# Modulation products of a two-block model move from the expert layer to two feed-forward layers

## Chip, cores and metric

The kernel runs on one core of a Trainium2 chip. The time is device microseconds of one execution, from its first to its last instruction with what lies around it; several executions are run and their median is given. Lower is better.

## What is computed

The reference runs two blocks over 256 tokens of 1024 features. The first block has two layers (attention, convolution, then a dense feed-forward in layer 0 and 8 routed experts in layer 1). The second block has two layers, and each of its steps is modulated by vectors that are made from two conditions, `c` for the tokens and `c_ctx` for a context of 256 tokens:

```python
silu_c = jax.nn.silu(c)
silu_cc = jax.nn.silu(c_ctx)
for i in range(DEPTH):
    m_lat = jnp.split((silu_c @ w_mod[i] + b_mod[i])[:, None, :], N_MOD, axis=-1)
    m_ctx = jnp.split((silu_cc @ w_mod[i] + b_mod[i])[None, None, :], N_MOD, axis=-1)
    h_lat = ffn_sublayer(h_lat, m_lat[0], m_lat[1], m_lat[2], ...)
    ...
```

`w_mod[i]` is 1024 x 9216 fp32 for each of the two layers, 75 MB together. It depends on nothing that the first block computes, so its products can stand anywhere before their first reader.

## The kernel before

Features lie on partitions, tokens on the free axis. The order of work is written out by hand, engine by engine, as a row of phases: `win0`, `proj0`, `wout0`, `ffn`, `win1`, `proj1`, `wout1`, `moe` (first block), then `fa0`, `naqkv`, `wo0`, `fb0`, `fa1`, `waqkv`, `wo1`, `fb1` (second block). Engines meet by semaphores only.

A phase is a row of steps. A step loads one weight tile of 128 x 2048 (an up step, gate and up of 128 hidden features, or any plain projection) or 128 x 1408 (a down step) by SyncE (SP) into one of four RAW slots. Each tile is cut in two pieces. ScalarE rounds a piece to fp32r (`high`, L1333, into WH), VectorE makes the rest (`low`, L1724, into WL), both two steps ahead of TensorE. TensorE multiplies three times for each block of 128 x 128 weights: high by high, low input by high weight, high input by low weight (`piece_product`, L936). An up step has 48 such products and a down step 33, of 256 columns (272 in `ffn`); steps of `fa0`, `fb0` and `fa1` that serve both streams have twice as many. `ffn` has 38 steps: two experts' worth of 11 up and 8 down steps. `moe` has 8 x 19 = 152. `fa0` and `fb0` have 65: 16 up steps of one stream, 3 up steps of both, 8 down steps of both (19 to 26), then 11 up and 8 down steps of each stream alone (27 to 45, 46 to 64).

`load` (L694) waits until VectorE has made the low part of the step four earlier, and SP issues its DMAs strictly in order. Results go to PSUM: `bank` gives a step one of four pairs of banks in turn, and `begin` makes TensorE wait until the former user of the pair is evacuated.

**The modulation.** `w_mod` is 72 tiles of 128 x 2048, 36 of each layer. `mod_product` (L977) multiplies a tile by the 2-column conditions SCF: 8 fp32 matmuls (16 records in the profile), at four column positions of the array in turn. The tiles stand beside experts 0 to 5 of `moe`, 12 beside each, in pairs behind the steps 1, 4, 7, 10, 13 and 16 of an expert (`mod_tiles`, `beside_moe`). One buffer is MRAW, the other TMP, and GpSimd loads them in a loop over the experts (L817), each when the product two tiles earlier is done (`s_mpc`). ScalarE copies the 2 x 4 result rows of a tile from PSUM to MROW (`mod_out`, L1395) and writes them to DRAM by four DMAs of 2 KB (L1398). In expert 6 ScalarE reads all 72 rows back (L1411), TensorE turns them by 16 transposes (`mod_turn`, L988), VectorE sums the four partial rows and the bias in four rounds (`mod_round`, L1785) and finishes them (`mod_finish`), and GpSimd makes the tables AB and GA of all five norms of the second block (`tables`).

Two more places matter. Between phases stands a layer norm: `norm` on TensorE sums over features by products with ONES (L1092, L1098). And norms of the second block are "hosted" by phases (`half_norm`, `half_sum`): beside steps 0 to 7 of `fa0`, 46 to 53 of `fa0` and so on, TensorE makes one product L1029 at the first of these steps and one L1032 at the third, which waits for GpSimd's sum of squares (L867). The routing of `moe` has 16 products of 8 columns at step 1 (L1008, 32 records) and 16 of 128 columns at each of the steps 5 and 7 (L1017).

Of the kernel before, what the change touches and what calls it, by code (L numbers as in the profile page):

```python
# [28 lines left out]
P = 128  # L29
# [39 lines left out]
MOD_EXPERTS = 6  # L69
MOD_PER_EXPERT = MOD_STEPS // MOD_EXPERTS  # L70
# [60 lines left out]
class Phase:  # L131
# [187 lines left out]
def build(nc, ins, out):  # L319
# [11 lines left out]
    with ctx:  # L331
# [16 lines left out]
        MLD = TMP[0:MOD_STEPS, :, :].rearrange("p a (b n) -> p (a b) n", b=2)  # L348
# [38 lines left out]
        MTILE = [MRAW[:, :], TMP[:, :, :].rearrange("p a b -> p (a b)")]  # L387
# [267 lines left out]
        def mod_rows_of(g, st, j):  # L655


            return PS[1 + 4 * (g // 2) + 2 * j][:, (2 * (g % 2) + st) * MOD_STEPS:(2 * (g % 2) + st + 1) * MOD_STEPS]
# [30 lines left out]
        def _(sp):  # L689
# [10 lines left out]

            def in_steps(name, e0):
                p = ph[name]
                for s, (t, e, k, _) in enumerate(p.steps):
                    load(p, s, ins["w_gu" if t == "u" else "w_dn"][e0 + e, k])

            def bias_tiles(layer):


                if layer == 0:
                    sp.wait_ge(s_browd, 32)  # L710
                sp.wait_ge(s_pc, ph[f"win{layer}"].p0)
# [55 lines left out]
        def _(pool):  # L767
# [44 lines left out]
            pool.wait_ge(s_pc, ph["moe"].p0)  # L812
            pool.wait_ge(s_ul, KC * (U_IDX["moe"] + 1))
# [17 lines left out]
            def tables():  # L831

                named = [hn for hn in halves if hn.half == 0]

                for hn in named:
                    t = (hn.layer * 72 + hn.idx * KC) // 2
                    for st in range(2):
                        sh = MOD[:, st, t:t + KC // 2, :].rearrange("p a b -> p (a b)")
# [4 lines left out]
                pool.wait_ge(s_tab, 10)  # L843
# [46 lines left out]
            pool.wait_ge(s_mod, 10)  # L890
            tables()
# [17 lines left out]
            for name in ("2n0", "2b0", "2a1"):  # L909
                two_halves(name)  # L910
# [4 lines left out]
        def _(pe):  # L915
# [54 lines left out]
            def mod_product(i, k):  # L970


                pe.wait_ge(s_mev, i * MOD_PER_EXPERT + k + 1)
                pe.wait_ge(s_mw[k % 2], (i * (MOD_PER_EXPERT // 2) + k // 2 + 1) * 16)
                for b in range(2):
                    for g in range(4):
                        last = pe.matmul(PS[1 + 2 * (k % 2)][32 * g:32 * g + 2, 0:256], SCF[:, 4 * b + g, :],  # L977
# [3 lines left out]
            def mod_turn():  # L981

                pe.wait_ge(s_mrl, 16)
                pe.wait_ge(s_mev, MOD_STEPS + 2)
# [7 lines left out]
            def beside_moe(i, s):  # L992


                if i < MOD_EXPERTS:
                    for k in mod_tiles(s):
                        mod_product(i, k)
                elif i == MOD_EXPERTS and s == 3:
                    mod_turn()
# [44 lines left out]
            def in_steps(name):  # L1044
# [4 lines left out]
                for s, (t, e, k, (c0, n)) in enumerate(p.steps):  # L1049
# [16 lines left out]
                    if name == "moe":  # L1066
# [1219 lines left out]
```

## Time and profile before

| | |
|---|---|
| median of 3 timed runs | 3238.85 us |
| lowest and highest of them | 3236.56, 3258.69 us |
| profiled execution, its own time | 3272.8 us |
| its span, first to last instruction | 3271.1 us |
| TensorE busy | 3160.7 us, 97% |
| VectorE, ScalarE, GpSimd busy | 1945.0, 1578.4, 392.3 us |
| mean granted TensorE clock | 0.987 |

The durations below are from the one profiled execution. Lines are those of the kernel before. PE is TensorE, PEld its weight loads, DVE VectorE, ACT ScalarE, POOL GpSimd, SP SyncE. A `q` behind an engine's name marks what its sequencer issues, such as a DMA. Products are pipelined: each record is about 0.28 us long, and one starts about every 0.12 us, so the distance from start to start is what a product costs.

### The profile page before, as it was taken

What the parts mean: (1) busy time and instruction counts of PE and PEld (TensorE: products, weight loads), DVE (VectorE), ACT (ScalarE), POOL (GpSimd) and SP (SyncE); (2) the same over time, 40 slices, a digit from 0 to 9 for tenths busy, and PEclk for the clock granted to TensorE, in tenths of its full rate; (3) what the DMA queues carried; (4) which work ended last, traced back from release to release, by engine and by line L of the source; (5) the groups of instructions that cost most, each with busy time, mean ns of one, the idle gap of its engine ahead of it and who ended that gap; (6) DMA issues with size and microseconds to landing.
All of it is one profiled execution on the core that took longest, in us unless ns stands there. A gap on an engine that the chain in (4) does not pass through costs nothing.

```text
span 3271.1 us, 63095 instructions
## 1 busy us (share of the span) xinstructions
PE 3160.7 (97%) x26594; PEld 3031.7 (93%) x26594; DVE 1945.0 (59%) x3076; ACT 1578.4 (48%) x2707; POOL 392.3 (12%) x482
## 2 busy tenths in 40 slices
PE   8999999999999999999999999999999999998998
PEld 7789998898889989999999997889999999996998
DVE  5965569645545555667357645584467635776554
ACT  4654455544444444455245546553355524556544
POOL 0000040000000000122001412150011400130000
PEclk9999999999999999999999999999999999999999
DMA  6335482367777787555245541243455424550352
GB/s 245 116 116 174 165 260 104 120 253 285 293 284 273 289 305 260 196 190 183 95 155 192 195 173 41 102 163 110 151 181 198 169 97 160 186 185 26 125 191 97
DMA packets 102866, 580.81 MB, mean 178 GB/s; under 512 B 16977, under 2 KB 25297, under 8 KB 49658
## 3 DMA queue, kind: packets, MB, share of 16 engines
q1 hardware_dynamic: 86176, 489.54, 42.2%
q0 software_dynamic: 13568, 84.91, 7.0%
q8 instruction: 211, 3.46, 0.4%
q10 hardware_dynamic: 2842, 2.34, 0.2%
q14 instruction: 69, 0.57, 0.0%
HBM read 575.08 MB, written 11.04 MB: 179 GB/s over the span
## 4 chain that ended last, share of the span: by engine, by line
PE 82%; DVE 9%; ACT 3%; DMA 2%; POOL 2%; issue 1%; ACTq 0%; POOLq 0%; SPq 0%; DVEq 0%
PE PS L936 73%; DVE CONV L2054 3%; DVE WL L1724 2%; PE PS L1218 2%; DMA TMP<-in_w_mod 2%; PE PS L977 2%; POOL TMP L867 1%; PE PS L1191 1%; PE PS L1205 1%; ACT WH L1333 1%; PE PS L1098 1%; PE PS L1092 1%; DVE NMX L1953 0%; DVE RSTD L1743 0%; DMA RAW<-in_w_in 0%
## 5 line engine op out<-in xcount | busy, mean ns | idle before, releaser
L1724 DVE TENSOR_TENSOR WL<-RAW,WH 128x1024 fp32r<-128x1024 f32 (+1 forms) x1018 | 1157.6, 1140 | 909.2 <-ACT WH L1333 902.3
L936 PE MATMUL PS<-UH,WH 128*128 128x256 f32 (+1 forms) x5536 | 1536.0, 284 | 24.8 <-DVE TMP L2114 7.8
L936 PE MATMUL PS<-UL,WH 128*128 128x256 f32 (+1 forms) x5536 | 1521.8, 281 | 0.0
L936 PE MATMUL PS<-UH,WL 128*128 128x256 f32 (+1 forms) x5536 | 1521.4, 281 | 0.0
L1333 ACT ACTIVATE WH<-RAW 128x1024 fp32r<-128x1024 f32 (+1 forms) x1018 | 982.5, 968 | 886.2 <-PE PS L936 865.3
L936 PEld LDWEIGHTS PS<-UH,WH 128*128 128x128 f32 x5536 | 1038.6, 190 | 41.9 <-issue 18.1
L936 PEld LDWEIGHTS PS<-UH,WL 128*128 128x128 f32 x5536 | 1034.6, 190 | 0.0
L936 PEld LDWEIGHTS PS<-UL,WH 128*128 128x128 f32 x5536 | 1033.6, 189 | 0.6
L936 PE MATMUL PS<-HIDH,WH 128*128 128x256 f32 (+1 forms) x2112 | 550.8, 281 | 0.0
L936 PE MATMUL PS<-HIDL,WH 128*128 128x256 f32 (+1 forms) x2112 | 548.4, 280 | 0.0
L936 PE MATMUL PS<-HIDH,WL 128*128 128x256 f32 (+1 forms) x2112 | 548.4, 280 | 0.0
L936 PEld LDWEIGHTS PS<-HIDH,WH 128*128 128x128 f32 x2112 | 381.4, 190 | 8.7 <-issue 6.5
L936 PEld LDWEIGHTS PS<-HIDL,WH 128*128 128x128 f32 x2112 | 380.4, 189 | 0.0
L936 PEld LDWEIGHTS PS<-HIDH,WL 128*128 128x128 f32 x2112 | 380.2, 189 | 0.0
L1468 ACT ACTIVATE SILHT<-PS 128x256 f32<-128x256 f32 (+2 forms) x255 | 99.3, 389 | 358.6 <-PE PS L936 358.5
L1890 DVE TENSOR_TENSOR SILHT<-SILHT,PS 128x256 f32<-128x256 f32 (+2 forms) x255 | 109.8, 431 | 217.8 <-ACT SILHT L1468 217.8
L1471 ACT ACTIVATE HIDH<-SILHT 128x256 fp32r<-128x256 f32 (+2 forms) x255 | 107.1, 420 | 19.4 <-DVE SILHT L1890 18.9
L1896 DVE TENSOR_TENSOR HIDL<-SILHT,HIDH 128x256 fp32r<-128x256 f32 (+2 forms) x255 | 116.2, 456 | 0.0
L856 POOL TENSOR_TENSOR TMP<-H 128x256 f32<-128x256 f32 x9 | 7.1, 790 | 846.4 <-DVE H L1837 823.4
L817 POOL DMA_DIRECT2D MRAW<-in_w_mod x36 | 19.1, 530 | 714.1 <-PE PS L977 551.7
L2054 DVE SCALAR_TENSOR_TENSOR CONV<-HPAD,VEC,CONV 128x272 f32<-128x272 f32 (+1 forms) x232 | 96.5, 486 | 0.0
L1837 DVE SCALAR_TENSOR_TENSOR H<-PS,MOD,H 128x256 f32<-128x256 f32 x128 | 58.6, 479 | 44.3 <-PE PS L936 44.3
(207 smaller groups left out, 2280.6 us busy)
## 6 DMA issues: line engine op xcount, KB each, us to landing
RAW<-in_w_gu SPq DMA_DIRECT2D x255, 1024.0 KB, 4.8
RAW<-in_w_dn SPq DMA_DIRECT2D x168, 704.0 KB, 4.1
MRAW<-in_w_mod POOLq DMA_DIRECT2D x36, 1024.0 KB, 7.0
TMP<-in_w_mod POOLq DMA_DIRECT2D x36, 1024.0 KB, 9.6
RAW<-in_w_in SPq DMA_DIRECT2D x30, 1024.0 KB, 8.0
RAW<-in_w_na SPq DMA_DIRECT2D x20, 1024.0 KB, 4.9
RAW<-in_w_o SPq DMA_DIRECT2D x12, 1024.0 KB, 4.8
RAW<-in_w_proj SPq DMA_DIRECT2D x8, 1024.0 KB, 4.9
```

What stands on the lines that cost most here:

```text
L867: pool.tensor_tensor(s2, s2, TMP[:, slot, at], ALU.add).then_inc(s_s2p, 1)
L936: last = pe.matmul(ps[:, a:b], w, m[:, a:b], start=first and a == 0, stop=final and b == n)
L977: last = pe.matmul(PS[1 + 2 * (k % 2)][32 * g:32 * g + 2, 0:256], SCF[:, 4 * b + g, :], MTILE[k % 2][:, (4 * b + g) * 256:(4 * b + g + 1) ...
L1218: last = pe.matmul(out, PT2[:, 2 * (g % 2) + half, x * P:(x + 1) * P], QKV[:, a.value0 + a.chunk(it), j * P + HD * half:j * P + HD * half ...
L1333: act.activation(WH[slot][:, 0:hi - lo], RAW[:, p.raw(s), lo:hi], ACT.Copy).then_inc(s_hi, 1)
L1468: act.activation(SIL[:, k % 2, 0:n], pair_banks(p, s)[0], ACT.Silu).then_inc(s_sil, 1)
L1471: act.activation(HIDH[:, k, hid_cols((c0, n))], HT[:, k % 2, 0:n], ACT.Copy).then_inc(s_hid, 1)
L1724: dve.tensor_tensor(WL[slot][:, 0:hi - lo], RAW[:, p.raw(s), lo:hi], WH[slot][:, 0:hi - lo].bitcast(F32), ALU.subtract).then_inc(s_lo, 1)
L1837: last = dve.scalar_tensor_tensor(x, ps[:, t0 - r[0]:t0 - r[0] + nt], mod(*gate, m, st), x, ALU.mult, ALU.add)
L1890: dve.tensor_tensor(HT[:, k % 2, 0:n], SIL[:, k % 2, 0:n], pair_banks(p, s)[1], ALU.mult).then_inc(s_evd, 1)
L1896: dve.tensor_tensor(HIDL[:, k, cols], HT[:, k % 2, 0:n], HIDH[:, k, cols].bitcast(F32), ALU.subtract).then_inc(s_hidl, 1)
L2054: own.inc(dve.scalar_tensor_tensor(y, x, tap, y, ALU.mult, ALU.add))
```

## The change

The 36 tiles of layer 0 now stand beside `ffn`, one behind each of its steps 1 to 36. The 36 tiles of layer 1 stand beside `fa0`, one behind a step, from step 22 on; where a down step serves one stream, the steps 1, 3 and 5 of the eight have none (and none is left for the last, 7, of the second stream). SP loads them, each behind the weight load of four steps later (`mod_load`). Their buffers are MRAW and CB (the router's weights, not in use in those phases); TMP is no longer one. In `ffn` the results go to banks 6 and 7, so the steps of `ffn` share three pairs of banks instead of four; in `fa0` they go to banks 1 and 3. TensorE waits for the last copy of layer 0 before the norm `b0`, which follows `ffn`.

The rows are turned per layer: ScalarE reads 36 of them back at step 19 of `moe` (expert 1) and at step 19 of `fb0`; TensorE turns them at step 22 by 16 products with the identity, which now add up the four partial rows in PSUM; VectorE adds the bias in two instructions and finishes five of the groups (`mod_sum`). GpSimd makes the tables of layer 0's three norms behind the first turn, and those of layer 1's two norms between the norms `2n0` and `2b0`. Waits are moved to match. The load loop on GpSimd is gone.

```diff
+MOD_LAYER = MOD_STEPS // 2
+MOD_FROM = {"ffn": 1, "fa0": 22}
+MOD_LOAD_LAG = 4
+MLD_STEP, TURN_STEP = {"moe": 19, "fb0": 19}, {"moe": 22, "fb0": 22}
...
+        if self.name == "ffn":
+            return 2 * (s % (BANK_SETS - 1))
...
-        MTILE = [MRAW[:, :], TMP[:, :, :].rearrange("p a b -> p (a b)")]
+        MTILE = [MRAW[:, :], CB[:, :, :].rearrange("p a b -> p (a b)")]
+        MLD = MRAW[0:MOD_LAYER, :].rearrange("p (b n) -> p b n", b=8)
...
-        def mod_tiles(s):
-            return (2 * (s // 3), 2 * (s // 3) + 1) if s % 3 == 1 and s < 18 else ()
+        def mod_steps(name):
+            steps = [(s, t, k, r) for s, (t, _, k, r) in enumerate(ph[name].steps) if s >= MOD_FROM[name]]
+            if name == "fa0":
+                steps = [x for x in steps if x[1] == "u" or x[3] == BOTH or x[2] not in (1, 3, 5)]
+            return [x[0] for x in steps[:MOD_LAYER]]
...
+        def mod_bank(k):
+            return PS[6 + k % 2] if k < MOD_LAYER else PS[1 + 2 * (k % 2)]
...
+            def mod_load(k):
+                if k == 0:
+                    sp.wait_ge(s_pc, ph["ffn"].p0)
+                if k == MOD_LAYER:
+                    sp.wait_ge(s_mrt, 1)
+                    sp.wait_ge(s_evd, ph["moe"].evacs("d", ph["moe"].n))
+                sp.wait_ge(s_mpc, k + 1)
+                sp.dma_start(MTILE[k % 2], ins["w_mod"][k]).then_inc(s_mw[k % 2], 16)
...
                 for s, (t, e, k, _) in enumerate(p.steps):
                     load(p, s, ins["w_gu" if t == "u" else "w_dn"][e0 + e, k])
+                    tile = mod_tile(name, s - MOD_LOAD_LAG)
+                    if tile is not None:
+                        mod_load(tile)
+                for s in range(p.n - MOD_LOAD_LAG, p.n):
+                    if mod_tile(name, s) is not None:
+                        mod_load(mod_tile(name, s))
...
-            with pool.Fori(0, MOD_EXPERTS) as i:
-                for k in range(MOD_PER_EXPERT):
-                    pool.wait_ge(s_mpc, i * MOD_PER_EXPERT + k + 1)
-                    pool.dma_start(MTILE[k % 2], ins["w_mod"][i * MOD_PER_EXPERT + k]).then_inc(s_mw[k % 2], 16)
...
-                for j in range(2):
-                    for g in range(4):
-                        for st in range(2):
-                            last = pe.transpose(mod_rows_of(g, st, j), MLD[:, 2 * g + st, j * P:(j + 1) * P],
-                                                IDENT[0:MOD_STEPS, 0:MOD_STEPS])
+                for g in range(4):
+                    for st in range(2):
+                        for j in range(2):
+                            last = pe.matmul(mod_rows_of(st, j), MLD[:, 2 * g + st, j * P:(j + 1) * P],
+                                             IDENT[0:MOD_LAYER, 0:MOD_LAYER], start=g == st == j == 0,
+                                             stop=g == 3 and st == j == 1)
...
+            def mods(name, s):
+                if mod_tile(name, s) is not None:
+                    mod_product(mod_tile(name, s))
+                if TURN_STEP.get(name) == s:
+                    mod_turn(int(name == "fb0"))
...
                 in_steps(nm)
                 if i == 0:
+                    pe.wait_ge(s_mev, MOD_LAYER + 2)
                     norm("b0", H, ONES, c0, n, s_evd, lambda c: ph[nm].evacs("d") - KC + c + 1)
```

How the order changes, at three places. First TensorE in the experts before: behind step 1 stand the router's products (L1008) and the first pair of tiles (L977, one from MRAW, one from TMP); the next pair stands three steps later.

```order
L936 MATMUL PS<-UL,WH 128x256
L936 MATMUL PS<-UH,WL 128x256
L1008 MATMUL PS<-RT,H 128x8 x16
L977 MATMUL PS<-MRAW,SCF 2x256 x8
L977 MATMUL PS<-TMP,SCF 2x256 x8
L936 MATMUL PS<-UH,WH 128x256
...
L936 MATMUL PS<-UH,WL 128x256
L977 MATMUL PS<-MRAW,SCF 2x256 x8
L977 MATMUL PS<-TMP,SCF 2x256 x8
L936 MATMUL PS<-UH,WH 128x256
```

In the changed kernel (where L936 is L971, L977 is L1012, L1008 is L1042, L1017 is L1051 and the turn is L1022) the tiles stand in `ffn`, one behind a step. The first two are these, from MRAW and from CB:

```order
L971 MATMUL PS<-UH,WL 128x272
L1012 MATMUL PS<-MRAW,SCF 2x256 x8
L971 MATMUL PS<-UH,WH 128x272
...
L971 MATMUL PS<-UH,WL 128x272
L1012 MATMUL PS<-CB,SCF 2x256 x8
L971 MATMUL PS<-UH,WH 128x272
```

In the experts the router's products are left with L971 on both sides; further on stand the routing's products at step 5 and the turn of layer 0.

```order
L971 MATMUL PS<-UH,WL 128x256
L1042 MATMUL PS<-RT,H 128x8 x16
L971 MATMUL PS<-UH,WH 128x256
...
L971 MATMUL PS<-UH,WL 128x256
L1051 MATMUL PS<-CST,STD 128x128 x4
L1051 MATMUL PS<-CST,RSTD 128x128 x4
L971 MATMUL PS<-UH,WH 128x256
...
L971 MATMUL PS<-UH,WL 128x256
L1022 MATMUL PS<-CST,MRAW 128x36 x16
L971 MATMUL PS<-UH,WH 128x256
```

So no tile is left in the experts, and each tile now has 33 to 96 products of L971 on either side instead of another tile on one.

The third place is SP's queue at `ffn`. Before, its loads of gate and up weights (`in_w_gu`), down weights (`in_w_dn`) and then those of `win1` (`in_w_in`) stand alone:

```order
L694 DMA RAW<-in_w_out 128x2048 x4
L694 DMA RAW<-in_w_gu 128x2048 x11
L694 DMA RAW<-in_w_dn 128x1408 x8
L694 DMA RAW<-in_w_gu 128x2048 x11
L694 DMA RAW<-in_w_dn 128x1408 x8
L694 DMA RAW<-in_w_in 128x2048 x9
```

Now (L714 is `load`, L730 `mod_load`) a tile stands behind each weight load from the sixth on, and four behind the last:

```order
L714 DMA RAW<-in_w_out 128x2048 x4
L714 DMA RAW<-in_w_gu 128x2048 x6
L730 DMA MRAW<-in_w_mod 128x2048
L714 DMA RAW<-in_w_gu 128x2048
L730 DMA CB<-in_w_mod 128x2048
...
L714 DMA RAW<-in_w_dn 128x1408
L730 DMA MRAW<-in_w_mod 128x2048
L730 DMA CB<-in_w_mod 128x2048
L730 DMA MRAW<-in_w_mod 128x2048
L730 DMA CB<-in_w_mod 128x2048
L714 DMA RAW<-in_w_in 128x2048 x9
```

The loads of `fa0` read alike from its step 26 on. SP takes them in this order only, so a weight load now also stands behind what the tile ahead of it waits for.

## Rows read from the trace of the kernel before

**Rows 1.** The page, engines and the chain by line.

```profile
PE 3160.7 (97%) x26594; PEld 3031.7 (93%) x26594; DVE 1945.0 (59%) x3076; ACT 1578.4 (48%) x2707; POOL 392.3 (12%) x482
...
PE PS L936 73%; DVE CONV L2054 3%; DVE WL L1724 2%; PE PS L1218 2%; DMA TMP<-in_w_mod 2%; PE PS L977 2%; POOL TMP L867 1%; PE PS L1191 1%; PE PS L1205 1%; ACT WH L1333 1%; PE PS L1098 1%; PE PS L1092 1%; DVE NMX L1953 0%; DVE RSTD L1743 0%; DMA RAW<-in_w_in 0%
```

**Rows 2.** Waits of the whole span (us in total, times, longest).

```profile
PE PS L977 <- DMA TMP<-in_w_mod: 11.3, 5, 2.7
...
PE PS L1032 <- POOL TMP L867: 12.5, 9, 1.5
```

**Rows 3.** Timeline, TensorE around one pair of modulation tiles (start us, us, engine line).

```profile
1023.30 1.04 PE L977 MATMUL PS<-MRAW,SCF 128*2 128x256 f32 x16
...
1024.16 1.05 PE L977 MATMUL PS<-TMP,SCF 128*2 128x256 f32 x16
...
1025.13 0.19 PEld L936 LDWEIGHTS PS<-UH,WH 128*128 128x128 f32 x1 [0.44 <-issue]
1025.14 0.38 PE L936 MATMUL PS<-UH,WH 128*128 128x256 f32 x1
```

**Rows 4.** The chain in order of time (start us, us, what).

```profile
238.22 192.90 PE PS L936 x1560
...
1004.99 1.84 PE PS L977 x32
...
1023.37 1.84 PE PS L977 x32
...
1310.44 163.29 PE PS L936 x1440
1487.12 268.55 PE PS L936 x2280
```

**Rows 5.** Windows with a low clock: stretch, busy us (instructions) by engine, PEclk, DMA share, GB/s.

```profile
660.80:664.20 3.40, 3.40 (x33) 1.08 (x32) 0.00 (x0) 0.00 (x0) 0.53 (x1) 0.50 0.88 316
753.00:756.40 3.40, 3.40 (x23) 2.01 (x23) 0.00 (x0) 0.00 (x0) 0.53 (x1) 0.50 1.00 342
964.60:968.00 3.40, 3.15 (x22) 1.77 (x23) 0.00 (x0) 0.00 (x0) 0.53 (x1) 0.50 0.94 301
1176.20:1179.60 3.40, 3.40 (x19) 3.36 (x16) 0.00 (x0) 0.00 (x0) 0.53 (x1) 0.50 0.96 366
```

**Rows 6.** Windows with the products of L936 alone.

```profile
757.00:774.50 17.50, 17.50 (x151) 1.00 0.74 271
777.00:792.50 15.50, 15.50 (x139) 1.00 0.77 280
969.00:986.00 17.00, 17.00 (x147) 1.00 0.74 274
989.00:1004.50 15.50, 15.50 (x140) 1.00 0.75 277
```

**Rows 7.** Timeline: the turn of before and the router's products.

```profile
657.19 3.63 PE L1008 MATMUL PS<-RT,H 128*128 128x8 f32 x32
...
1309.26 1.18 PE L988 MATMUL PS<-CST,TMP 72*128 72x72 f32 x16
```

**Rows 8.** Windows: the kernel's first loads.

```profile
4.00:14.00 10.00, 5.36 (x16) 4.20 (x16) 1.33 (x2) 3.29 (x3) 0.00 (x0) 1.00 1.06 408
```

**Rows 9.** DMA issues (KB each, median us to landing).

```profile
RAW<-in_w_gu SPq DMA_DIRECT2D x255, 1024.0 KB, 4.8
RAW<-in_w_dn SPq DMA_DIRECT2D x168, 704.0 KB, 4.1
...
TMP<-in_w_mod POOLq DMA_DIRECT2D x36, 1024.0 KB, 9.6
```

**Rows 10.** Timeline: the end of ffn.

```profile
430.96 1.31 PE L1092 MATMUL PS<-H,ONES 128*128 128x272 f32 x5
431.16 1.06 ACT L1333 ACTIVATE WH<-RAW 128x1024 fp32r<-128x1024 f32 x1 [0.73 <-PE PS L936]
```

**Rows 11.** Instructions of line L1395 (duration ns min/median/max).

```profile
L1395 ACT ACTIVATE MROW<-PS x72: 360/383/396, 673.6 to 1286.6; 128x256 f32<-128x256 f32 x72
```

More of the change, by code:

```diff
@@ L710, in bias_tiles @@
                     sp.wait_ge(s_browd, 32)
+                else:
+                    for b in range(2):
+                        sp.wait_ge(s_mr[b], MOD_LAYER // 2 * 64 + 16)
                 sp.wait_ge(s_pc, ph[f"win{layer}"].p0)
@@ L829, in modulate, with tables @@
                     last.then_inc(s_um, 1)
-            def tables():
-                named = [hn for hn in halves if hn.half == 0]
+            def tables(layer):
+                named = [hn for hn in halves if hn.half == 0 and hn.layer == layer]
                 for hn in named:
@@ L888, in two_halves @@
                         half_residual(hn)
-            pool.wait_ge(s_mod, 10)
-            tables()
+            pool.wait_ge(s_mod, 5)
+            tables(0)
             for c in range(KC):
@@ L908, in _ @@
                 pool.tensor_tensor(nbv, nbv, mask, ALU.add).then_inc(s_nb, 1)
-            for name in ("2n0", "2b0", "2a1"):
-                two_halves(name)
+            two_halves("2n0")
+            pool.wait_ge(s_mod, 10)
+            tables(1)
+            two_halves("2b0")
+            two_halves("2a1")
             modulate("fb1", "2n1", 1, 6, SEQ)
@@ L1065, in in_steps @@
                             piece_product(p, s, h, [(PS[p.bank(s)][:, 0:n], terms, h == 0, h == 1)], part)
-                    if name == "moe":
-                        if s < KH:
-                            routing(s)
-                        beside_moe(*expert_step(s))
+                    if name == "moe" and s < KH:
+                        routing(s)
+                    mods(name, s)
                     hn, j = hosted(p, s)
@@ L1473, in in_steps @@
                         ahead(p, s)
-                    if name == "moe":
-                        if s < KH:
-                            routing(s)
-                        beside_moe(*expert_step(s))
+                    if name == "moe" and s < KH:
+                        routing(s)
+                    mods(name, s)
+                    if name == "moe" and expert_step(s)[0] == N_EXP - 1:
+                        context_input(expert_step(s)[1])
                     hn, j = hosted(p, s)
@@ L1764, in low_u @@
                 return (3 if modulated else 2), make
-            def mod_round(g):
-                if g == 0:
-                    dve.wait_ge(s_mrt, 1)
-                else:
-                    dve.wait_ge(s_dve, mod_rounds[-1])
-                for st in range(2):
-                    for j in range(2):
-                        base = MOD[:, st, :, j] if g else VEC[:, V_BM + j:V_BM + 2 * MOD_STEPS:2]
-                        own.inc(dve.tensor_tensor(MOD[:, st, :, j], mod_rows_of(g, st, j), base, ALU.add))
-                mod_rounds.append(own.value)
@@ L1779, in mod_finish, with mod_sum @@
[L1779 to L1800 removed]
+            def mod_sum(layer):
+                dve.wait_ge(s_mrt, layer + 1)
+                tiles = slice(layer * MOD_LAYER, (layer + 1) * MOD_LAYER)
+                bias = VEC[:, V_BM + layer * 2 * MOD_LAYER:V_BM + (layer + 1) * 2 * MOD_LAYER].rearrange("p (t j) -> p t j", j=2)
+                for st in range(2):
+                    rows = PS[1][:, 2 * st * MOD_LAYER:2 * (st + 1) * MOD_LAYER].rearrange("p (j t) -> p t j", j=2)
+                    last = dve.tensor_tensor(MOD[:, st, tiles, :], rows, bias, ALU.add)
+                link(last)
+                for idx in (1, 4, 7, 2, 8):
+                    m = MOD[:, :, layer * 36 + idx * 4:layer * 36 + idx * 4 + 4, :]
+                    dve.tensor_scalar(m, m, *((1.0, None, ALU.add) if idx in (1, 4, 7) else (0.5, None, ALU.mult)))\
+                        .then_inc(s_mod, 1)
@@ L1801, in beside_moe, with mods, context_input @@
+            def mods(name, s):
+                if TURN_STEP.get(name) == s - 1:
+                    mod_sum(int(name == "fb0"))
+            def context_input(s):
+                if 2 <= s <= KC + 1:
                     c = s - 2
@@ L1918, in in_steps @@
                             ahead(p, s, (1,))
-                    if name == "moe":
-                        if s < KH:
-                            routing(s)
-                        beside_moe(e, s % (KH + KC))
+                    if name == "moe" and s < KH:
+                        routing(s)
+                    mods(name, s)
+                    if name == "moe" and e == N_EXP - 1:
+                        context_input(s % (KH + KC))
                     if hn:
@@ L2153, in _ @@
             in_steps("fb0", (0, 8), 6)
+            dve.wait_ge(s_mod, 10)
             in_steps("fa1", (1, 2), 8)
```

101 lines of the change are left out of this document (41 added, 60 removed).

## The prediction

> **What bounds the kernel now.** I read the page first. TensorE is busy 97% of the span, and in the chain that ended last the products of the three-term weight scheme (PE L936) alone hold 73%. Beside them the same row has two entries of the modulation: 2% in which the chain runs through "DMA TMP<-in_w_mod", 2% for the products L977 [rows 1]. So the question is what the modulation costs TensorE where it stands now and where it will stand. The waits say that TensorE really stood still for a modulation tile only 5 times, 11.3 us in all [rows 2]. The chain in order of time gives the rest. A pair of tiles recurs every three steps: one begins at 1004.99, the next at 1023.37, 18.38 us for 144 products of L936 and the pair [rows 4]. Where no modulation stands between, 1440 products take 163.29 us, 113.4 ns each [rows 4], so 144 are 16.33 us and a pair costs 2.05 us.
>
> The timeline shows what these 2.05 us are made of [rows 3]: 0.86 us from the first tile's start (1023.30) to the second's, 0.98 us from the second's start until L936 goes on at 1025.14, and the other 0.21 us ahead of the first. The weight loads stood idle for 0.44 us before L936's first one. The 0.21 and what is over 0.86 in the 0.98 belong to the change of kind, not to the tile. A pair pays it once.
>
> By the Trainium skill (TensorE: Matmul & The Clock Gate, Part 3: Packing small matmuls) a weight load runs beside products in flight only where it uses other rows of the array; these tiles use all 128, so a group has to drain. This trace agrees, with its 0.44 us. The rule speaks against splitting pairs.
>
> Two more things are read from the windows. The granted clock was 0.50 for 3.4 us at 753.0, 964.6 and 1176.2, each time at a late tile, and at 660.8, right after the 32 short products of the router, L1008 [rows 5, 7]. The other two of the five late tiles were not followed by a low clock. And L936 has two spacings at full clock: 151 in 17.5 us (116 ns) from 757.0, then 139 in 15.5 us (111.5 ns as counted) after the next pair; 147 in 17.0 from 969.0, then 140 in 15.5 [rows 6]. On long stretches these are 113.4 ns [rows 4] and 268.55/2280 = 117.8 ns, in fa0 [rows 4]. Both times the wide spacing ended at a modulation group; nothing else stood there.
>
> **The change, part by part.** All 72 tiles remain, with the same 16 recorded products each, but every one stands alone: 36 behind steps 1 to 36 of ffn, 36 behind steps of fa0. A tile alone costs 0.21 + 0.98 = 1.19 us. The bounds are half a pair, 1.03 us, and a whole pair, 2.05 us; I take 1.19, since both its parts are measured.
>
> 1. Experts (moe). 36 pairs leave: 36 x 2.05 = 73.8 us. The waits go, 11.3 us [rows 2], with three stretches of 3.4 us at half clock, 1.7 us each, 5.1 us [rows 5], and the wide spacing after two of them, some 155 products x 4.4 ns each, 1.4 us. Together -91.6 us. The half clock at 660.8 follows L1008, which stays: it will now lie on L936 at about the same price, 0. What can be late next in the experts is nothing that the trace shows: weights land in 4.8 and 4.1 us [rows 9] and have some three steps.
>
> 2. The turn. 16 transposes with one record each took 1.2 us [rows 7]. Now 16 true fp32 products stand in each of two turns. The nearest row is L1008, 16 such products with 128 weight columns, 32 records, 3.6 us [rows 7]; the bound below is the transposes' 1.2 us. I take 3.6 us each: in moe -1.2 + 3.6 = +2.4, in fb0 +3.6. L1008 was followed by a half clock; for one of the two turns I count 1.7 us (bounds 0 and 3.4).
>
> 3. ffn. 36 x 1.19 = +42.8 us. No product of L936 waits there now (192.90 us for 1560, 123.7 ns [rows 4]), so nothing of it lies under a wait. If a group ends the wide spacing here too, 1536 products go from 123.7 to 113.4 + 16/2.4 = 120.1 ns (16 columns more at 2.4 GHz): -5.5 us; bounds -5.5 and 0. I take -5.5, since two of two did so. The three bank pairs instead of four cost nothing: VectorE empties a bank during the next step, two before it is needed.
>
> 4. The end of ffn. TensorE must now see the last tile's copy before the norm b0. ScalarE makes that copy behind its last weight part, which starts at 431.16 and takes 1.06 us [rows 10]; the copy takes 0.38 us [rows 11]. With the two hand-overs between the engines the sums for the norm begin at about 432.8 instead of 430.96 [rows 10]: +1.8 us, all on the path.
>
> 5. fa0. 36 x 1.19 = +42.8 us. One wait of about 1.4 us for GpSimd's sums (12.5 us in 9, [rows 2]), behind step 48, is covered by the three groups before it: -1.4. From step 22 to the wait at step 48 the spacing is wide in the row of 2280; 1248 products x 4.4 ns = -5.5 us if a group ends it. In fb0 the turn might do the same, another -5.5 us; a turn isn't a modulation group, and I count nothing.
>
> 6. The loads. They leave GpSimd's queue for SP's, each behind the weight load of four steps later. SP reaches it about 2 us into the interval after step x-2, since that weight load waits for VectorE's part of step x. What is then queued: a tile behind a weight load. Alone they land in 4.8 us (1024 KB) and 4.1 us (704 KB) [rows 9], and the stream moved 408 GB/s while the first loads of the kernel were queued [rows 8], so 1.05 MB more take 2.6 us: 7.4 us behind an up load, 6.7 behind a down load. The time there is until the product: two steps and two groups less 2 us. In up steps of ffn (48 x 123.7 = 5.9 us) 12.2 us, in down steps (33, 4.1 us) 8.5 us. In the down steps of fa0, 3.74 us at 113.4 ns, with one group between, 6.7 us: three tiles behind up loads are late by 0.7 us. I take +1 us (0 to 3). ffn asks 1.77 MB in 5.27 us in its down steps, 336 GB/s, below the 408. SP's wait for the product before the last one holds up weights only at the end, where win1's first has a norm's time.
>
> The Trainium skill (DMA: Bandwidth & Descriptors, Specifications) gives about 358 GB/s as one core's share of HBM; the trace had 408, so the measurement decides. With 358 a tile would land 0.4 us later, which makes eight tiles in fa0's down steps late by 0.4 us more, some 3 us by an estimate from that page.
>
> GpSimd's loop goes at no gain, as it is waited for only through its loads. The table work splits in two, each several steps ahead of its reader. VectorE's sums shrink from 16 to 4 and lie beside TensorE. ScalarE copies the same 72 rows; one per step is less at a time.
>
> Sum: moe -91.6 + 2.4 = -89.2; ffn +42.8 - 5.5 + 1.8 = +39.1; fa0 +42.8 - 1.4 - 5.5 = +35.9; fb0 +3.6; turn's clock +1.7; late tiles +1.0. That is -7.9 us. The profiled execution took 3272.8 us, so 3265; it was 1.0% above the median of the timed runs, 3238.85, where the same difference gives 3231. A measurement of this kernel can tell about 1% (32 us) from no change, so I call it the same.
>
> **The rivals.**
> A. A lone group drains no worse than its half of a pair, and the turns keep the clock and close up fb0: 72 x 0.16 = 11.5, 1.7 and 5.5 us less, -26 us, 3212. For it: the mean over all the pairs. Against it: the 0.44 us idle before every return to L936.
> B, the slower side. The modulation groups are what puts the expert stream into its narrow spacing, and without them it stays wide from the half clock at 660.8 on: 6240 products x 4.4 ns = +27 us, and if groups don't close up ffn and fa0 either, +11 us. Together +31 us, 3270. It decides at the first product behind L1008's half clock. For it: both changes from wide to narrow came at such groups. Against it: the routing's products (L1017) and the turn also break the stream, within 25 us, and the spacing stayed narrow for 163 us with no group in it.
> C. Tiles come late in the queue they now share with the weights: if the second load lands in 9.6 us, as TMP's tiles did from GpSimd's queue [rows 9], 16 down steps of ffn and 9 of fa0 wait 1.1 to 2.9 us each, and a late tile can cost 1.7 us in clock. 25 x 2.5 = +62 us, 3293. Against it: 9.6 us was the second of two tiles beside weights, under an issuing loop.
> D. The change doesn't do what it says: waits remain in moe for another reason. Then -7.9 + 17.8 = +10 us, 3249.
>
> **How the numbers follow.** My forecast 0.53, A 0.15, B 0.17, C 0.10, D 0.05. Below 3206 lies only the tail of A with more gain than I can name, 0.07. Above 3271 lie C and half of B's spread with the timing's own (the three runs went to 3258.69): 0.15. The rest, 0.78, is within 1%. The range 3206 to 3272 holds A, B and D. The likeliest case's own is 3222 to 3243.
>
> **What would show it.** In the changed profile: no wait of the tile products in moe; moe shorter by 89 us; lone groups every 7.1 us in ffn, 1.19 us each in the chain; L936 near 120 ns in ffn and 113.4 in fa0 behind step 22; a norm b0 that starts 1.8 us after the last product; turns of 3.6 us. Wrong would be: tile products waiting for DMA in down steps (C), 117.8 ns through the experts (B), lone groups at 1.03 us (A), or a half clock that recurs in ffn.

## The result and the profile after

| | before | after |
|---|---|---|
| median, us | 3260.58 (16 runs, 3236.56 to 3285.67) | 3274.92 (16 runs, 3257.86 to 3298.77) |
| profiled execution, us | 3272.8 | 3264.8 |
| its span, us | 3271.1 | 3262.9 |

The ratio is 1.0053, with a 95% interval of 1.0028 to 1.0079; it is worked out without one run of before, 3285.67 us, which counts as slow, and the medians of the table alone differ by 14 us. The change costs 0.5%, about 17 us (9 to 26), where the forecast had a gain of 7.9. It lies within 1%, as the likeliest class said, but on the other side of 1, and 3275 lies above the range. Of the 44 us between 3231 and 3275 half is not the change: the kernel before, run 16 times beside the changed one, has a median 22 us above that of the three runs which the forecast started from.

The two profiled executions alone would say the opposite, since the one after is 8.2 us shorter. So the first thing to read is the page, and then the stretches that the change touches.

The page after: engines, the chain by line, DMA issues.

```profile
PE 3158.6 (97%) x26642; PEld 3018.8 (93%) x26642; DVE 1945.3 (60%) x3064; ACT 1577.8 (48%) x2707; POOL 360.8 (11%) x410
...
PE PS L971 74%; DVE CONV L2090 3%; DVE WL L1769 2%; PE PS L1251 2%; PE PS L1012 2%; PE PS L1224 1%; POOL TMP L899 1%; PE PS L1238 1%; DMA MRAW<-in_w_mod 1%; ACT WH L1367 1%; PE PS L1131 1%; PE PS L1125 1%; DVE NMX L1989 0%; DVE RSTD L1788 0%; DMA RAW<-in_w_in 0%
...
RAW<-in_w_gu SPq DMA_DIRECT2D x255, 1024.0 KB, 4.8
RAW<-in_w_dn SPq DMA_DIRECT2D x168, 704.0 KB, 4.1
MRAW<-in_w_mod SPq DMA_DIRECT2D x36, 1024.0 KB, 7.5
CB<-in_w_mod SPq DMA_DIRECT2D x36, 1024.0 KB, 7.0
```

L936 is now L971, and L977 is L1012. Against [rows 1], the modulation's transfer has gone from 2% of the chain to 1%, the products' share has stayed at 2%. TensorE is as busy as before.

The waits after:

```profile
PE PS L1066 <- POOL TMP L899: 11.5, 9, 1.5
...
PE PS L1012 <- DMA MRAW<-in_w_mod: 5.2, 4, 2.1
...
PE PS L1125 <- ACT MROW L1429: 1.4, 1, 1.4
```

Against [rows 2], 11.3 us of waiting for tiles in the experts are gone, and 5.2 us of a new kind are there, in ffn and fa0. The wait at the norm b0 is the third line.

Windows from the first product of ffn, moe, fa0 and fb0 to the first of the phase behind it (columns as in [rows 5]), before and then after:

```profile
234.63:444.77 210.14, 207.63 (x1649) 205.29 (x1649) 116.83 (x162) 100.78 (x150) 3.72 (x9) 1.00 0.51 175
645.14:1468.10 822.96, 810.74 (x7568) 761.79 (x7569) 446.56 (x676) 373.80 (x580) 69.97 (x129) 0.99 0.70 260
1468.10:1842.36 374.26, 371.51 (x3178) 370.91 (x3177) 218.46 (x296) 168.53 (x250) 42.59 (x44) 1.00 0.47 163
2133.96:2516.47 382.51, 374.82 (x3179) 373.85 (x3177) 227.72 (x309) 173.35 (x258) 61.87 (x61) 0.99 0.45 156
```

```profile
235.60:491.83 256.23, 250.44 (x2224) 218.82 (x2225) 116.69 (x162) 110.52 (x186) 3.56 (x9) 1.00 0.77 288
691.92:1430.46 738.54, 737.97 (x6432) 737.05 (x6433) 449.50 (x657) 353.62 (x508) 29.29 (x43) 0.99 0.53 186
1430.46:1841.70 411.24, 406.13 (x3754) 377.27 (x3753) 215.54 (x296) 178.01 (x285) 46.27 (x44) 1.00 0.65 241
2133.20:2517.74 384.54, 376.82 (x3211) 375.64 (x3210) 228.28 (x316) 173.29 (x258) 65.33 (x75) 0.98 0.45 156
```

The first number behind each window is its length. In this pair the four stretches grow by 0.7 us in all, while the span shrinks by 8.2: stretches that the change does not touch differ by some 9 us. That happens between executions of one kernel too: the second block's fa1 lasted from 368.8 to 377.6 us over four executions of the kernel before. A single pair of profiles can't judge a change of this size by its span; the touched stretches over several can. Each kernel was profiled four times (this run and three more each). Mean length, us:

| stretch | before (lowest to highest) | after | difference | forecast |
|---|---|---|---|---|
| ffn | 210.1 (all) | 256.3 (255.1 to 257.1) | +46.2 | +39.1 |
| moe | 820.7 (818.2 to 823.0) | 738.6 (all) | -82.2 | -89.2 |
| fa0 | 369.9 (364.1 to 374.3) | 413.2 (411.2 to 415.1) | +43.3 | +35.9 |
| fb0 | 382.0 (381.7 to 382.5) | 385.1 (382.0 to 389.6) | +3.0 | +3.6 |
| turn's clock, late tiles | | | in the rows above | +2.7 |
| sum | | | +10.3 | -7.9 |

+10.3 lies inside the timing's 9 to 26. The whole spans of the same eight profiles don't: their means are 3263.5 before and 3265.7 after, only 2.2 us apart, above all since fa1 took 365.8 to 366.1 us in all four profiles after, 8.0 less on the mean. The products of fa1 are the same in both kernels, and in lag3 and expert_groups, whose fa1 is that of the changed kernel, it took 374.7 and 374.9; whether the change has a part in it is not shown. So the account that follows is one of the touched stretches, +10.3 against -7.9, 18 us of error, and not of the whole time.

### The profile page after: what moved, and what is told of

It is laid out like the page before. It is cut to its first block, busy times and chain, and to the rows that moved or that the text cites. A ratio compares the mean times of both kernels' runs of the same rounds, so it can differ in the third digit from the quotient of the medians.

```text
span 3262.9 us, 62962 instructions
## 1 busy us (share of the span) xinstructions
PE 3158.6 (97%) x26642; PEld 3018.8 (93%) x26642; DVE 1945.3 (60%) x3064; ACT 1577.8 (48%) x2707; POOL 360.8 (11%) x410
## 4 chain that ended last, share of the span: by engine, by line
PE 83%; DVE 9%; ACT 3%; POOL 1%; DMA 1%; issue 1%; ACTq 0%; SPq 0%; POOLq 0%; DVEq 0%
PE PS L971 74%; DVE CONV L2090 3%; DVE WL L1769 2%; PE PS L1251 2%; PE PS L1012 2%; PE PS L1224 1%; POOL TMP L899 1%; PE PS L1238 1%; DMA MRAW<-in_w_mod 1%; ACT WH L1367 1%; PE PS L1131 1%; PE PS L1125 1%; DVE NMX L1989 0%; DVE RSTD L1788 0%; DMA RAW<-in_w_in 0%
## 5 line engine op out<-in xcount | busy, mean ns | idle before, releaser
L971 PE MATMUL PS<-UH,WH 128*128 128x256 f32 (+1 forms) x5536 | 1534.5, 283 | 24.3 <-DVE TMP L2150 7.8
L971 PE MATMUL PS<-UL,WH 128*128 128x256 f32 (+1 forms) x5536 | 1518.0, 280 | 0.0
L971 PE MATMUL PS<-UH,WL 128*128 128x256 f32 (+1 forms) x5536 | 1517.5, 280 | 0.0
L971 PEld LDWEIGHTS PS<-UH,WH 128*128 128x128 f32 x5536 | 1036.5, 190 | 50.3 <-issue 26.6
L971 PEld LDWEIGHTS PS<-UL,WH 128*128 128x128 f32 x5536 | 1038.2, 190 | 0.6
L971 PEld LDWEIGHTS PS<-UH,WL 128*128 128x128 f32 x5536 | 1036.4, 190 | 0.0
L971 PE MATMUL PS<-HIDH,WH 128*128 128x256 f32 (+1 forms) x2112 | 547.2, 280 | 0.0
L971 PE MATMUL PS<-HIDL,WH 128*128 128x256 f32 (+1 forms) x2112 | 543.8, 278 | 0.0
L971 PE MATMUL PS<-HIDH,WL 128*128 128x256 f32 (+1 forms) x2112 | 543.6, 278 | 0.0
L971 PEld LDWEIGHTS PS<-HIDH,WH 128*128 128x128 f32 x2112 | 378.1, 188 | 13.2 <-issue 6.6
L971 PEld LDWEIGHTS PS<-HIDL,WH 128*128 128x128 f32 x2112 | 378.5, 188 | 0.0
L971 PEld LDWEIGHTS PS<-HIDH,WL 128*128 128x128 f32 x2112 | 378.1, 188 | 0.0
L1514 ACT ACTIVATE HIDH<-SILHT 128x256 fp32r<-128x256 f32 (+2 forms) x255 | 106.9, 419 | 10.7 <-DVE SILHT L1925 10.3
L1251 PE MATMUL PS<-QKV,PT 128*128 128x64 f32 x640 | 79.4, 277 | 1.0 <-DVE OS L2054 0.9
```

What stands on the lines that cost most here:

```text
L971: last = pe.matmul(ps[:, a:b], w, m[:, a:b], start=first and a == 0, stop=final and b == n)
L1251: last = pe.matmul(out, PT2[:, 2 * (g % 2) + half, x * P:(x + 1) * P], QKV[:, a.value0 + a.chunk(it), j * P + HD * half:j * P + HD * half ...
L1514: act.activation(HIDH[:, k, hid_cols((c0, n))], HT[:, k % 2, 0:n], ACT.Copy).then_inc(s_hid, 1)
```

## The experiments

The theory at this point: lone groups cost what was forecast, but the spacing of L971 doesn't narrow at them, and tiles come late more often. The rivals: B (the experts stay wide), C (late tiles decide), and that the turns cost the rest.

**Both kernels once more.** No edit.

> The changed kernel once more, for a second profile. Spacing theory (the change's own costs come to about nothing, and the median is 17 us worse because the expert stream, without its pairs of tiles, now often stays in the wide spacing of 117.8 ns instead of 113.3): moe differs from the first profile's 738.5 us by up to 27 us, the time stays 10 to 25 us above before. Cost theory (late tiles and half clocks cost more in most executions than in the first profile): moe again 735 to 742 us, but more than 5 us of waits of tile products, or more half clocks, in ffn and fa0.

> The kernel before once more, for a second profile and as a measure of the noise. Ratio 1.000 within 0.004. Spacing theory: moe again within 5 us of 823, since a pair of tiles every three steps brings L936 back to 113.3 ns; the phases without pairs (ffn, fa0, fb0, fa1, fb1) differ from the first profile by 5 to 15 us each, one way or the other. Cost theory: those phases agree within 2 us.

After: 3271.41 us, ratio 1.0060 (1.0031 to 1.0088). Before: 3262.52 us, 1.0024 (0.9995 to 1.0054) against itself, in the same session. So 0.3% is what this measurement can give for no change. The cost of the change shows twice, but against the second build of before, measured beside it, it is 0.3% (9 us) and no more. Two further profiled executions of each filled the table above.

> The changed kernel a third time, for its profile. Spacing theory: moe between 738 and 766 us, in steps that stand with the spacing of L971 (wide 117.8, narrow 113.3 ns). Cost theory: 738 us again.

> The kernel before a third time, for its profile. If the 12 us of the median that the profiles do not show lie in the spacing of phases which the change touches, some profile of before has ffn below 207 us or fa0 below 368 us (narrow). If not, ffn 210, moe 822, fa0 374 and fb0 382 come again within 1 us each.

> The changed kernel a fourth time, for its profile. If its experts are wide in some executions, moe is above 745 us in one profile of four; if not, 738.5 us again, and the four phases of the change (ffn, moe, fa0, fb0) sum to 1790 to 1797 us again.

> The kernel before a fourth time, for its profile; expected as for the third.

They took 3263.91 and 3266.67 us after, 3266.77 and 3251.95 before. moe was 738.5 to 738.6 us in all four profiles of after, so wide experts don't explain them.

**No tiles at all** (no_tiles). The 72 loads, products and copies are left out; the turned rows come from weights, so the modulation isn't computed.

```diff
-                    tile = mod_tile(name, s - MOD_LOAD_LAG)
-                    if tile is not None:
-                        mod_load(tile)
...
-                if mod_tile(name, s) is not None:
-                    mod_product(mod_tile(name, s))
```

> The changed kernel without the 72 tiles: no loads, no products, no copies of them; the rows that are turned come from the weights instead (this part of the computation is left out). Direct costs are 72 x 1.19 = 86 us, 5 us of late tiles, 1.4 us at the norm. Spacing theory: moe can be wide in all or most of its length, up to 745 us or more, so the time is only 75 to 95 us below the changed kernel's. Cost theory: 105 us or more below it, since tiles cost more than their groups, and moe is 735 to 742 us.

3176.04 us, ratio 0.9761 (0.9719 to 0.9804). The 72 tiles cost some 80 us where they stand before and some 95 where they stand after. In the profile ffn took 210.15, fa0 367.21, fb0 385.50, but moe 762.20 us, 23.7 more than after, although nothing of the tiles stands in moe in either kernel. The chain in order of time, no_tiles (L965 is L971) and then after, has the reason:

```profile
697.72 70.67 PE PS L965 x600
768.38 4.12 PE PS L1016 x32
772.50 633.52 PE PS L965 x5355
```

```profile
746.33 70.67 PE PS L971 x600
817.00 4.19 PE PS L1022 x32
821.19 614.90 PE PS L971 x5400
```

Both were wide (117.8 ns) on the 600 products behind the routing (L1051 after). After the turn one went on at 118.3 ns each, the other at 113.9. So B's wide experts exist; its price, 27 us, was about right. But this profiled execution was the slowest of its six, 26 us above their median, so the others were probably narrow (an estimate; they have no trace). And the changed kernel, which has no tiles in its experts either, was narrow behind the turn in all four profiles, with moe at 738.5 to 738.6 us. So taking the tiles out of the experts does not by itself leave them wide. That a few of the timed executions of after were wide is not excluded.

**A group in each later expert** (expert_groups). After, and behind step 1 of experts 1 to 7 eight small products of constants, of the tiles' shape, into a free bank.

```diff
+                    if name == "moe" and s >= KH + KC and s % (KH + KC) == 1:
+                        for b in range(2):
+                            for g in range(4):
+                                pe.matmul(PS[3][32 * g:32 * g + 2, 0:256], SCF[:, 4 * b + g, :],
+                                          CST[:, C_COS:C_COS + 256], start=b == 0, stop=b == 1)
```

> The changed kernel with one lone group of 8 small products, like a tile's but from a constant, behind step 1 of experts 1 to 7. Their price is 7 x 1.19 = 8.3 us. Spacing theory: the groups bring the stream to the narrow spacing, so moe is 745 to 750 us in the profile with no part of an expert wide behind its group, and the time is equal to the changed kernel's or up to 15 us below it. Cost theory: 8 us slower than the changed kernel, 25 us above before.

3291.27 us, ratio 1.0121 (1.0078 to 1.0165). The profile has moe at 743.35, 4.8 us over after: seven groups at 1.19 us are 8.3, and 3.5 came back, since the 600 products behind the routing were narrow (2.6 us) and no low clock followed the turn. The experts were narrow before their first group came, so the run prices the groups but doesn't test whether a group ends a wide stretch. The timing is some 20 us above that of after (ratio 1.0121 against 1.0060 in the same session), and the profile has as much: its span, 3284.6 us, is 18.9 above the mean of after. Beside moe's 4.8 it is fa1 with 9.0, fa0 with 4.4, fb0 with 2.8 and the part behind fa1 with 2.9, all with the instructions of after. The other five timed runs, 3279 to 3303 us, lie about as high; why is open.

**Layer 1's tiles in the experts** (layer1_experts). Layer 0's stay in ffn, layer 1's stand alone behind every third step of moe from step 26, with TMP as the second buffer.

```diff
-MOD_FROM = {"ffn": 1, "fa0": 22}
+MOD_FROM = {"ffn": 1, "moe": 26}
...
-            if name == "fa0":
-                steps = [x for x in steps if x[1] == "u" or x[3] == BOTH or x[2] not in (1, 3, 5)]
+            if name == "moe":
+                steps = steps[::3]
```

> One part of the change alone, in another place: layer 0's tiles stay beside ffn, layer 1's 36 lone tiles stand behind every third step of the experts (from step 26, buffers MRAW and TMP) instead of beside fa0. The number of lone groups, the turns and the norm's wait are those of the changed kernel. Spacing theory: a group every 17 us holds the experts at 113.3 ns, fa0 is free again; with the late tiles and the half clock of fa0 gone as well (about 5 us) the time is 8 to 20 us below the changed kernel's. Cost theory: 5 us below it, no more.

3304.45 us, ratio 1.0141 (1.0104 to 1.0179). fa0 went to 364.18, but moe to 827.37. The waits have the cause:

```profile
PE PS L1018 <- DMA TMP<-in_w_mod: 17.5, 10, 3.1
PE PS L1018 <- DMA MRAW<-in_w_mod: 17.0, 10, 2.8
```

These lines hold 1.9 us of two late tiles in ffn; in moe it is 32.6 us in 18 places. 36 lone groups (42.8) and these waits are 75 of the 89 us. The rest fits six stretches of 3.4 us at the lower clock behind late tiles (10 us) and some 580 more wide products (2.5). No theory had this. With each tile's load queued behind the weight load of four steps later, as in the changed kernel, tiles were late in 18 of 36 places of moe, though moe had half as many of them as before. It fails as a test of the spacing, but it shows what the place in the queue costs.

**The turn cut in four** (turn_spread). Its 16 products in four groups behind steps 22 to 25.

```diff
-                if TURN_STEP.get(name) == s:
-                    mod_turn(int(name == "fb0"))
+                if name in TURN_STEP and 0 <= s - TURN_STEP[name] < 4:
+                    mod_turn(int(name == "fb0"), s - TURN_STEP[name])
```

> The changed kernel with each turn's 16 products cut into four groups of 4, behind four steps in a row. Both theories: the half clock of 6.8 us that followed each turn (3.4 us lost each) is gone, and three more drains come per turn (0.3 us each): 4 to 7 us below the changed kernel in the profile. If the half clock comes without the burst too, the time is equal or 2 us worse.

Windows at the two turns of after. The first turn runs from 816.93 to 821.19 us, over the first line and into the second, the other from 2298.76 to 2303.42:

```profile
816.55:819.95 3.40, 3.40 (x31) 3.26 (x31) 2.01 (x4) 1.63 (x3) 0.00 (x0) 1.00 0.47 200
819.95:823.35 3.40, 3.40 (x17) 3.33 (x17) 0.01 (x1) 0.00 (x0) 0.00 (x0) 0.51 0.76 270
823.35:826.75 3.40, 3.40 (x18) 3.40 (x17) 0.00 (x0) 0.05 (x1) 0.00 (x0) 0.50 0.09 39
826.75:830.15 3.40, 3.40 (x32) 3.40 (x31) 1.34 (x2) 1.62 (x3) 0.00 (x0) 0.99 0.02 5
...
2301.30:2304.70 3.40, 3.40 (x17) 3.33 (x17) 0.00 (x0) 0.00 (x0) 0.00 (x0) 0.52 0.86 304
2304.70:2308.10 3.40, 3.40 (x18) 3.40 (x18) 0.00 (x0) 0.00 (x0) 0.00 (x0) 0.50 0.03 10
```

TensorE never paused, yet the granted clock was 0.50, the lower of its two levels (1.2 GHz), for 6.8 us from the last part of each turn on, and each such window of 3.4 us holds 17 or 18 products instead of 31 or 32. With the turn cut, the four groups took 1.08 us each, no low clock followed, moe took 734.39 us (738.6 after) and fb0 382.07 (385.1).

That is not all the clock's. The chain of turn_spread at the place where after had 70.67 us for 600 products:

```profile
747.37 68.02 PE PS L971 x600
```

They were narrow, 2.6 us less, ahead of the first turn. fb0 also took 382.0 in one profile of after, with its turn whole. The turn by itself is better taken from L971's starts on both sides, less the products between at their own spacing. In the profiles of the 32-record turn that is 7.05 us where 6.8 us of low clock followed, 5.5 where 3.4 did, and 3.9 in the two of 16 turns where none did (one in expert_groups, one in no_tiles). Cut in four it is 4.9. So the low clock costs a turn 3.2 or 1.6 us, and cutting it saves 2.2 or 0.6. In the timing, 1.0049 (1.0021 to 1.0077), that can't be told from after.

**The loads one step earlier** (lag3). Each tile's load stands in SP's queue behind the weight load of three steps later instead of four.

```diff
-MOD_LOAD_LAG = 4
+MOD_LOAD_LAG = 3
```

> The changed kernel with MOD_LOAD_LAG 3 instead of 4: each tile is loaded behind the weight load of three steps later, so SP issues it as soon as the product two tiles back is done, and no longer behind the weight load of a step later. If the late tiles of ffn and fa0 (4 to 5 waits, 5 us) come from the place in SP's queue, they fall under 1 us in the profile and the half clock that followed one in fa0 goes; 3 to 8 us below the changed kernel. If the DMA engines are what is short, the waits stay at 4 us or more, and weights may be late as well.

No wait of L1012 for a transfer is left, against 5.2 us after. The same window, after and then lag3:

```profile
1731.30:1734.70 3.40, 3.40 (x19) 3.40 (x18) 0.00 (x0) 0.00 (x0) 0.00 (x0) 0.51 0.95 373
```

```profile
1731.30:1734.70 3.40, 3.40 (x36) 2.69 (x37) 2.42 (x5) 1.99 (x5) 0.00 (x0) 1.00 0.98 386
```

After a tile waited for 2.1 us, the clock was at its lower level; in lag3 it stayed full. fa0 took 405.81 us (413.2 after), ffn 254.18 (256.3). That is 9.5 us, but in two of the four profiles of after the 1176 products ahead of fa0's first tile were wide, 2.6 us on the mean, and in lag3 they were not. Some 7 us are left for the late tiles with what follows them. The timing, 1.0051 (1.0018 to 1.0084), doesn't separate lag3 from after, so this number rests on one profile against four.

The window also bears on bandwidth: 386 GB/s. The Trainium skill (DMA: Bandwidth & Descriptors, Specifications) has about 358 for one core; this trace, like the one in [rows 8], lies above it.

**The pairs stay, SP loads them** (pairs_sp). The kernel before, with its tiles' loads moved from GpSimd's loop into SP's stream, each behind the weight load of three steps after its product's.

```diff
+                    if name == "moe":
+                        i, x = divmod(s - 3, KH + KC)
+                        if s >= 3 and i < MOD_EXPERTS:
+                            for k in mod_tiles(x):
+                                mod_load(i * MOD_PER_EXPERT + k)
...
-            with pool.Fori(0, MOD_EXPERTS) as i:
-                for k in range(MOD_PER_EXPERT):
-                    pool.wait_ge(s_mpc, i * MOD_PER_EXPERT + k + 1)
-                    pool.dma_start(MTILE[k % 2], ins["w_mod"][i * MOD_PER_EXPERT + k]).then_inc(s_mw[k % 2], 16)
```

> The kernel before with one thing changed: SP loads the modulation tiles, each pair behind the weight load of step s + 3 after the pair at step s, instead of GpSimd's loop. Pairs, turn and tables are those of before. If the 17.8 us of late tiles and low clock were GpSimd's queue, the waits of L977 fall from 11.3 us to under 2 us and the time is 10 to 18 us below before; if the three down steps (11.4 us) are too short for two tiles on any queue, the waits stay above 8 us.

3235.07 us, ratio 0.9918 (0.9885 to 0.9952): 27 us below the kernel before (16 to 37), and the fastest kernel here that leaves nothing out. Its waits have no line of a tile's product, and moe takes 804.95 us against 820.7, 15.8 less. The other 11 us of the timing aren't found there. In this one profile stretches without a change were shorter too: fb0 took 376.29 against 382.0, by a narrow spacing, fa1 368.9 against 373.9. So the edit's own share is the 15.8. The same stretch of the chain, before and then pairs_sp (L936 is L943, L977 is L984):

```profile
736.22 1.02 PE PS L977 x16
738.73 14.07 DMA TMP<-in_w_mod
752.93 1.88 PE PS L977 x16
754.81 20.01 PE PS L936 x162
```

```profile
736.19 1.84 PE PS L984 x32
738.03 11.44 PE PS L943 x99
749.47 1.84 PE PS L984 x32
751.30 18.58 PE PS L943 x162
```

The pair that waited for TMP at 752.93 starts at 749.47. Of the waits, the low clocks and the wide stretches that the change wanted to remove from the experts, worth 17.8 us in the forecast, nearly all came from where the load was queued, and could be had without moving a product. The run changes the queue and the place in the order at once; which of the two did it is not told apart.

## Why the prediction was wrong

Steps 3, 5, 6 and 2 of the forecast failed. The narrower spacing in ffn (-5.5) was seen in none of 14 profiles; that in fa0 (-5.5) came to about -2.5 on the means of four profiles each (some 1310 products of fa0 wide before, 750 after); late tiles took some 7 us and not 1; the two turns with their clock took 13 us and not 8.9. The rest are 2.3 and 2.6 us in the experts, and a narrower fb0 took some 3 us back by luck.

**Right.** A lone group costs 1.19 us. The timeline after, in ffn:

```profile
262.49 0.28 PE L971 MATMUL PS<-UH,WL 128*128 128x272 f32 x1
262.70 1.05 PE L1012 MATMUL PS<-MRAW,SCF 128*2 128x256 f32 x16
263.68 0.39 PE L971 MATMUL PS<-UH,WH 128*128 128x272 f32 x1
```

0.98 us from the group to L971, and 0.21 ahead of it where the spacing is 0.12. In every place with no wait and no other product beside the group it was so within 0.02 us, which refutes A. A lone group costs 0.16 us more than half a pair, 12 us over 72, so the tiles cost 85.7 us where the pairs cost 73.8. The Trainium skill (TensorE: Matmul & The Clock Gate, Part 3: Packing small matmuls) says that a weight load overlaps products in flight only where it uses other rows. The forecast made of it that such a group has to drain, and the price came out. The rule doesn't explain the price, though: L971's own weight loads use all 128 rows and do run beside its products, with PEld busy 93% of the span and PE 97%. D fell as well: no tile is waited for in moe. The wait at b0 was 1.4 us of the 1.8.

**Step 3, the spacing in ffn (-5.5): wrong.** It rested on two cases in [rows 6], in which a wide stretch ended at a pair, and it took ffn's 123.7 ns for a wide spacing. The chain after, in ffn and in fa0:

```profile
249.55 6.12 PE PS L971 x48
256.65 6.12 PE PS L971 x48
...
1618.45 5.66 PE PS L971 x48
1625.08 5.66 PE PS L971 x48
```

From start to start L971's products in ffn stand 122 to 125 ns apart, in after as in before; 120.1 was forecast. In none of the 14 profiles did products of 272 columns, undisturbed, have another spacing: only those of 256 columns show two, and no row of the trace before had said otherwise. So there was nothing for a group to end. 42.8 + 1.4 + 2.0 of late tiles are the 46.2 us measured.

Among products of 256 columns, a pair of before met a wide spacing 7 times in four profiles, and a narrow one followed each time. A lone group of after met one 12 times in its four, and it stayed wide 6 times. So what held for pairs did not carry over to lone groups; why is open. Behind a product that waits for GpSimd's sums (L1032, L1066) a narrow spacing turned wide in 41 of 119 cases, over all 14 profiles. The spacing may change at such breaks in either direction.

**Step 5, the spacing in fa0 (-5.5): the number came in one profile, the mechanism didn't.** In the profile after, fa0 was narrow from long before its first tile group at 1582.78:

```profile
1449.49 133.29 PE PS L971 x1176
```

That is 113.3 ns, where before had 117.8 in this stretch [rows 4]. No group ended a wide spacing there. In two other profiles of after fa0 was wide up to its first tiles and turned narrow behind the second or third, as forecast, and there it took 415.0 and 415.1 us.

Against the profile that the forecast was built on, fa0 grew by 37.0 us, and 36.9 were forecast with the late tiles. That agreement is luck, two misses in one: narrow throughout, fa0 is 10.1 us shorter and not 5.5 (364.1 against 374.3), and late tiles took 5 and not 1. And two of the four profiles of before had a narrow fa0 already, at least in large part, 364.1 and 367.0 us. On the mean most of the gain was not the change's. 364.1 + 42.8 - 1.0 (the wait that the groups cover) gives 405.9, and lag3, narrow and without late tiles, had 405.8.

**Step 6, late tiles (+1.0): mis-sized.** C's mechanism is real, but at 4 to 6 us of waits in 3 to 6 places and some 7 with the clock, not 62. The chain after, at the longest wait in ffn (1.5 us) and in fa0 (2.1):

```profile
330.22 9.77 DMA MRAW<-in_w_mod
...
1721.57 8.29 DMA MRAW<-in_w_mod
```

I took 7.4 us for a tile behind an up load. The four late ones took 7.8 to 9.8 us, where the forecast had 8.5 us to spare in ffn and 6.7 in fa0.

**Step 2, the turns: mis-sized.** They took 4.4 and 4.8 us from the last product ahead to the first behind, forecast 3.6 each, and in all four profiles both were followed by a low clock. With it they cost 7.05 us where it lasted 6.8 us and 5.5 where it lasted 3.4, 13 us for the two on the mean, where 8.9 in all was counted. fb0 came out at +3.0 with +3.6 forecast, but by luck: its turn cost 6.7 us on the mean, with the clock, and its products were narrower than before in three of four profiles, which the forecast named and counted at nothing.

**Step 1, the experts: nearly right.** moe came out at -82.2. The forecast -89.2 used the profile whose moe was the longest of four, 2.3 us above their mean; the turn with its clock took 2.8 us more on the mean than the 2.4 counted there, and 600 wide products behind the routing 2.6. That is 7.7 us, close to the 7.0 that were missing.

**The base.** The three runs ahead of the forecast gave 3238.85, sixteen gave 3260.58. The profiled execution was 1% above the three, and is 0.4% above the sixteen. The forecast noted the gap and scaled it away; the profiled time was the better base. With the sixteen as the base the forecast's own difference gives 3253, so the rest of the miss, 22 us in the medians, is the change's part: the steps above have 18 of it in the touched stretches.

## What to carry to other kernels

Read why a product waits before moving it: here the waits came from the queue and the place of a load in it, and moving 72 loads (15.8 us less in the experts) gained what moving 72 products did not. Keep small products of another shape together: each return to the wide ones costs, and splitting 36 pairs cost 12 us in lone groups. And judge a change of less than 1% by the stretches that it touches, over several profiles of both kernels, since a stretch may differ by 10 us with nothing changed. Then look at the whole spans as well: here they had 2.2 us where the touched stretches had 10.3, and the difference has to be said.

## What the runs showed of the hardware

- The same fp32r products of 256 columns run at 113.4 or 117.8 ns at a granted clock of 1.00, for hundreds of microseconds at a time; over 5400 products that was 23.7 us between no_tiles and after. Those of 272 columns had one spacing, 122 to 125 ns, in all 14 profiles. What sets it stays open.
- A dense burst of 16 products with few moving columns (3.7 to 5.0 us in the turn, [rows 7] for the router) was followed by a granted clock of 0.50 in 14 of 16 turns and behind the router in all 14 profiles, though the engine was never idle. Cut in four bursts of 1.1 us, it wasn't in any of 8.
- Open is also why the untouched stretches differ as they do between kernels: fa1 at 365.8 to 366.1 us in four profiles of after, 368.8 to 377.6 in four of before.
